# One inference step of a hybrid decoder on one core: a fifth staging place for the sample attention, and its third batch of keys staged with the first two

## The chip, the core and the metric

The kernel runs on one core of a Trainium2 chip. Its engines are named as in the profile: PE (TensorE, matrix products and transposes into PSUM), DVE (VectorE), ACT (ScalarE), POOL (GpSimd, here the issuer of gathers and of some loads) and SP (SyncE, here the issuer of the weight loads). They run in parallel, each in its own program order, and meet only at semaphores. The metric is the device time of one execution in microseconds; less is better.

## The reference

One layer of a decoder trunk for a prompt of 256 positions and for 8 sample rows of 4 new positions each: mixers, cross-attention, a mixture of experts. The change lies in the sparse attention of the sample rows. Each sample batch has 1024 cached positions in 8 pages, 2 key/value heads of 128, 8 query heads:

```python
def dsa_sample(q, k_new, v_new, qi, wi, ki_new, cache_k, cache_v, cache_idx_k, page_table, rel_bias):
    ...
    sc = indexer_scores(qi, wi, ki_all)
    sc = jnp.where(jnp.arange(n_keys)[None, None, :] <= qpos[None, :, None], sc, -jnp.inf)
    _, sel = lax.top_k(sc, topk)                      # 256 of the 1028 keys of each query
    ...
    k_sel = jnp.where(is_past, cache_k[phys, off], gather_rows(k_new, sn).astype(cache_k.dtype))
    v_sel = jnp.where(is_past, cache_v[phys, off], gather_rows(v_new, sn).astype(cache_v.dtype))
    rel_b = rel_bias[t5_bucket(qpos[None, :, None] - sel)]
    return sparse_attend(q, k_sel, v_sel, rel_b, valid)

def sparse_attend(q, k_sel, v_sel, rel_b, valid):
    ...
    logits = jnp.einsum('bqkgd,bqskd->bqkgs', qg, k_sel).astype(jnp.float32) * (Dh ** -0.5)
    logits = logits + rel_b...
    p = jax.nn.softmax(jnp.where(valid, logits, -jnp.inf), axis=-1).astype(v_sel.dtype)
    o = jnp.einsum('bqkgs,bqskd->bqkgd', p, v_sel)
```

The output of the attention goes, with the mixer's, into one output projection; cross-attention and the experts follow. All is in float32.

## The kernel before, in words

All work is written out by hand, engine by engine; there is no scheduler. PE runs the input projection in 12 items (`products(n)`, L711), with the prompt's attention and the indexer woven between its tiles (`INSIDE`, `AFTER`), then the sample attention, the output projection (L1023), the cross-attention, the router and the experts. SP loads the weights in the order of use, each into a place of a ring when PE has freed it.

The sample attention does not select keys: it computes the scores of all 1028 keys of a batch and adds a bias that holds the relative bias and, from the top-k rounds on DVE, a large negative value for keys not chosen. It works in two halves (`x` = 0, 1) of four batches:

- POOL gathers a batch's keys or values (128 x 2048 floats, 1 MB) from the paged cache into a staging place with an indirect DMA (`gather`, L584). There are four places of 2048 columns, `staged(b)` L333: two in `stageM`, two in `stageK`; batch b + 4 takes the place of batch b, and values 0 to 3 take the places of batches 4 to 7. Values 4 to 7 go to `vn_`, `qT_`, `qiT_` and `Kt` (L345), which are read by other work before; `qT_`, `qiT_` and `Kt` hold turned keys until the second half's scores are done. `stageK` lies in `nT`, the normed input, and is free when the last item's products are done.
- PE turns a batch's keys with 16 transposes of 128 x 128, in four groups of four (one PSUM bank each), and ACT (L1799) and DVE (L2181) copy two banks each to `keys_t(b)`. A group waits until its bank is copied out (`kt_free` counts ACT's copies, `kt_laid` DVE's, `kt_ready` PE's groups). Batches 0 and 1 are turned early, by `first_keys` (L870, transposes at L876), between the last steps of the last item (`AFTER[N_OUT - 1]`); their copies all go to DVE (L2156).
- PE computes the scores of four batches in PSUM (L979, releases `s_qk`), adds the bias (L986, releases `s_logits`; the first half waits for DVE's `topkS`). DVE takes the maximum (L2185), ACT the exponential (L1802, L1808), DVE scales and masks (L2190, L2191, releases `s_probs`).
- PE turns the probabilities (L996, L998) in banks 6 and 7, ACT copies them out (L1813, L1815), PE multiplies by the values (L1007, waits `v_in0`/`v_in1` for four gathers each; releases `s_o`), turns the result (L1013), and ACT lays it for the output projection (L1823). PE does this for half 0 and then half 1, after the scores of both.

POOL's order is one loop over b = 0 to 11 (keys of 8 batches, values of the first four): b = 2 waits for the last item's products (`ring_free`), b of 4 and more for the transposes of the batch whose place it takes, and the values of batch 4 go before b = 6. The last three gathers (values 5, 6, 7) wait for `s_qk` 2, the scores of both halves. Then POOL loads `xts` (L609, L611) and the memory keys. The tensor `nine` (4096 columns) holds the prompt's memory values in columns 0 to 1023 and is otherwise unused until the experts' ring takes it.

## Time and profile before

| | |
|---|---|
| three runs | 1218.6 us median (1215.48, 1218.6, 1225.76) |
| profiled execution | 1216.17 us; its span from first to last instruction 1214.3 us |
| busy in the span | PE 1131.3 us (93%), DVE 472.5, ACT 185.8, POOL 48.7 |
| chain that ended last, by engine | PE 79%, DVE 9%, DMA 7%, ACT 3% |
| of it, by line | L711 21%, L1023 15%, L1301 13%, DMA of `in_w_up` 5%, DMA of `in_cache_v` 1% |
| mean granted clock of TensorE | 0.977 |

The span has four stretches: the input projection with the prompt's attention up to 452 us; the sample attention, 452 to 497; output projection, cross-attention and router, 497 to 728, with a mean DMA share of 0.51; and the experts, 728 to 1204, with a DMA share of 0.99 at 415 GB/s. A row of the trace names start and duration in us, engine, line, operation, output and inputs by tile, partitions x elements, and in brackets the idle time of the engine before it and what released it. PE's matmul durations overlap; their ends are modelled.

### The profile page before, as it was taken

To read this page: it belongs to the slowest core of one execution; us is meant where nothing else is said; L and a number is where in the kernel's file an instruction comes from. 1 tells how busy PE (TensorE), PEld (TensorE's weight loads), DVE (VectorE), ACT (ScalarE), POOL (GpSimd) and SP (SyncE) were. 2 spreads that over 40 slices of the span, in tenths; PEclk is the share of its full clock that TensorE was granted. 3 is DMA by queue.
4 is the path that set the end of the run, shared out by engine and by line. 5 is a ranking of instruction groups with operands and counts; after the bars stand their busy time and mean duration, and the time that the engine had idled before them with its cause. 6 is when DMAs were issued, how large, how long until landed. Compare 5 with 4: busy or idle time off the path is not lost.

```text
span 1214.3 us, 14024 instructions
## 1 busy us (share of the span) xinstructions
PE 1131.3 (93%) x5834; PEld 557.4 (46%) x5834; DVE 472.5 (39%) x968; ACT 185.8 (15%) x399; POOL 48.7 (4%) x63
## 2 busy tenths in 40 slices
PE   7999999999999989899999899899999999859985
PEld 4334343344444455677777564333333333323332
DVE  5000069199564664011112466233333333412342
ACT  2103123200231343000012422000000000000010
POOL 0002000000000012100001001000000000000000
PEclk9999999999999999999999999899999999989998
DMA  8835623555343358744455739999999999999996
GB/s 292 294 122 136 190 73 124 191 174 173 109 134 104 109 206 320 291 136 137 138 171 184 286 119 405 399 412 426 428 426 427 427 426 427 426 426 428 425 427 245
DMA packets 71084, 327.60 MB, mean 270 GB/s; under 512 B 14006, under 2 KB 17878, under 8 KB 54444
## 3 DMA queue, kind: packets, MB, share of 16 engines
q1 hardware_dynamic: 55152, 282.65, 59.4%
q0 software_dynamic: 7888, 37.06, 8.1%
q10 hardware_dynamic: 7980, 6.99, 2.3%
q8 instruction: 47, 0.77, 0.3%
q14 instruction: 17, 0.14, 0.0%
HBM read 318.45 MB, written 10.49 MB: 271 GB/s over the span
## 4 chain that ended last, share of the span: by engine, by line
PE 79%; DVE 9%; DMA 7%; ACT 3%; issue 1%; POOL 0%; DVEq 0%; SPq 0%; ACTq 0%
PE PS L711 21%; PE PS L1023 15%; PE PS L1301 13%; PE PS L1383 7%; DMA ring<-in_w_up 5%; PE PS L1262 4%; PE PS L684 3%; PE PS L1308 2%; DVE X L2065 2%; DVE top L2064 2%; PE PS L1360 1%; PE PS L1266 1%; PE PS L1376 1%; DMA X<-in_cache_v,ids 1%; PE PS L705 1%
## 5 line engine op out<-in xcount | busy, mean ns | idle before, releaser
L711 PE MATMUL PS<-ring,NC 128*128 128x512 f32 x704 | 320.8, 600 | 1.8 <-issue 1.8
L711 PEld LDWEIGHTS PS<-ring,NC 128*128 128x128 f32 x704 | 128.7, 191 | 153.6 <-issue 152.0
L1023 PE MATMUL PS<-NC,ring 128*128 128x288 f32 x768 | 189.9, 407 | 1.6 <-DVE X L2223 0.5
L1301 PE MATMUL PS<-ring,NC 128*64 128x512 f32 x560 | 163.7, 605 | 7.7 <-DMA ring<-in_w_up 7.2
L1023 PEld LDWEIGHTS PS<-NC,ring 128*128 128x128 f32 x768 | 144.6, 190 | 42.4 <-issue 2.1
L2416 DVE TENSOR_TENSOR X<-X,PS 128x1024 f32<-128x1024 f32 x52 | 63.5, 1221 | 119.0 <-PE PS L1262 119.0
L1301 PEld LDWEIGHTS PS<-ring,NC 128*64 128x64 f32 x560 | 46.2, 138 | 101.6 <-issue 100.1
L1262 PE MATMUL PS<-XNN,NC 64*128 64x512 f32 x208 | 58.8, 642 | 1.4 <-DVE XNN L2454 0.8
L2223 DVE TENSOR_TENSOR X<-X,PS 128x288 f32<-128x288 f32 x16 | 7.3, 454 | 117.9 <-PE PS L1023 117.9
L1308 PE MATMUL PS<-ring,NC 128*32 128x256 f32 x384 | 35.8, 449 | 16.5 <-DMA ring<-in_w_up 14.9
L1909 ACT ACTIVATE NC<-PS,small 64x512 f32<-64x512 f32 x11 | 7.5, 680 | 273.6 <-PE PS L1301 239.7
L2064 DVE MAX8 top<-X 32x8 f32<-32x1028 f32 (+2 forms) x48 | 44.7, 931 | 1.0
L2065 DVE MATCH_REPLACE8 X<-top,X 32x1028 f32<-32x1028 f32 (+2 forms) x48 | 43.9, 914 | 0.0
L2419 DVE TENSOR_TENSOR X<-X,PS 32x1024 f32<-32x1024 f32 x26 | 31.5, 1210 | 26.6 <-PE PS L1266 26.4
L2091 DVE TENSOR_TENSOR ring<-small,cst 128x128 f32<-128x128 f32 x1 | 0.3, 293 | 105.1 <-ACT small L1636 105.1
L1383 PE MATMUL PS<-ring,NC 128*64 128x512 f32 x176 | 39.4, 595 | 0.0
L684 PE MATMUL PS<-ring,NC 128*32 128x512 f32 x288 | 38.4, 605 | 0.0
L1308 PEld LDWEIGHTS PS<-ring,NC 128*32 128x32 f32 x384 | 18.1, 128 | 34.7 <-issue 29.8
L1262 PEld LDWEIGHTS PS<-XNN,NC 64*128 64x128 f32 x208 | 15.8, 186 | 39.5 <-issue 25.6
L2454 DVE COPY XNN<-PS 128x1024 f32<-128x1024 f32 x11 | 13.5, 1225 | 44.6 <-PE PS L1383 32.1
L1830 ACT ACTIVATE NC<-X,gcol 128x288 f32<-128x288 f32 x16 | 8.6, 535 | 117.0 <-DVE X L2223 117.0
L630 POOL DMA_INDIRECT NC<-nsc,tabS x13 | 13.0, 1002 | 331.1 <-PE PS L1253 281.6
(454 smaller groups left out, 1178.5 us busy)
## 6 DMA issues: line engine op xcount, KB each, us to landing
ring<-in_w_gate SPq DMA_DIRECT2D x27, 2048.0 KB, 20.0
ring<-in_w_up SPq DMA_DIRECT2D x22, 2048.0 KB, 17.1
ring<-in_w_in SPq DMA_DIRECT2D x36, 1024.0 KB, 5.1
ring<-in_w_down SPq DMA_DIRECT2D x16, 2048.0 KB, 18.5
ring<-in_w_out SPq DMA_DIRECT2D x16, 1024.0 KB, 5.1
nine<-in_w_down SPq DMA_DIRECT2D x6, 2048.0 KB, 22.1
XNN<-in_w_up SPq DMA_DIRECT2D x5, 2048.0 KB, 18.9
NC<-in_w_gate SPq DMA_DIRECT2D x5, 2048.0 KB, 20.8
```

What stands on the lines that cost most here:

```text
L684: last = mm(acc(n, 2)[32 * k:32 * k + 32, 0:width], lhs[:, 4 * q + k, T:NT], ws[:, k, 0:width], start=st, stop=sp_)
L711: last = mm(acc(n, t)[:, 0:width], lhs[:, kt, t * 128:(t + 1) * 128], slot(m)[:, k, 0:width], start=kt == 0, stop=kt == KT - 1)
L1023: last = mm(PS[:, j, 0:NT], slot(m)[:, k, 128 * j:128 * j + 128], src[:, kt, :], start=kt == 0, stop=kt == width * 4 - 1)
L1262: last = mm(PS[:, banks + half, :], slot_w[rows, k, 128 * t:128 * t + 128], ysb[rows, k, 512 * x:512 * x + 512], start=True, stop=True)
L1301: last = mm(PS[64 * half:64 * half + 64, 2, :], x[:, kt % 8, kt // 8, :], weights[half][:, kt % 8, :], start=kt == 0, stop=kt == KT - 1)
L1308: last = mm(PS[32 * c:32 * c + 32, bank, 0:256], x[:, kt % 8, kt // 8, STRIP * sub:STRIP * sub + STRIP], weights[c // 2][:, kt % 8, 256 * ...
L1383: last = mm(PS[64 * half:64 * half + 64, bank + x, :], hT[:, f, :], w[:, f % 2, half * 1024 + x * 512:half * 1024 + x * 512 + 512], start= ...
L2064: own(V.max(best, work))
L2065: own(V.match_replace(work, best, work, TAKEN))
L2416: return TT(out, out, PS[:, banks:banks + 2, :], ALU.add)
L2419: last = TT(out, out, PS[32 * x:32 * x + 32, banks:banks + 2, :], ALU.add)
L2454: V.tensor_copy(ysb[:, block_of(p) % 2, :], PSF[:, 2048:3072]).then_inc(S("y_out_psum"), 1)
```

## The change

- `KV_PLACES`: five staging places instead of four; the new one is `nine[:, 1024:3072]`. Key batch j takes place j % 5, the values of batches 0 to 3 take the next ones, and values 5 take the place in `nine`, 6 and 7 take `qT_` and `qiT_`; `Kt` holds no values any more.
- POOL gathers three batches of keys before it waits for `ring_free`, in the order keys 0 to 7, values 0 to 3, values 5; each from the sixth on waits for the transposes of the batch five before it. Keys 7 count on the semaphore `idx_in`. Two gathers (values 6, 7) are left behind `s_qk` 2.
- `first_keys(2)` turns the third batch between the fold of the last item and that item's transposes. Its four groups go to ACT. So the loop of the stage has one batch less in the first half.
- `turn_probs(x)` is the code of the probability transposes as a function; that of half 0 runs before the scores of half 1, after a wait for all DVE key copies (`kt_laid` 18).

```diff
@@ -332,9 +332,11 @@
...
+        KV_PLACES = (stageM[:, 0:2048], stageM[:, 2048:4096], nine[:, 1024:3072], stageK[:, 0:2048], stageK[:, 2048:4096])
+
         def staged(b):
...
-            return (stageM, stageK)[b % 4 // 2][:, 2048 * (b % 2):2048 * (b % 2) + 2048]
+            return KV_PLACES[b % 5]
@@ -342,7 +344,7 @@
...
-            return staged(b) if b < 4 else (vn_, qT_, qiT_, Kt)[b - 4]
+            return staged(8 + b) if b < 4 else (vn_, staged(12), qT_, qiT_)[b - 4]
@@ -588,20 +590,22 @@
...
-            for b in range(12):
-                if b == 2:
+            for j in range(13):
+                if j == 3:
                     pool.wait_ge(S("ring_free"), 4 * N_OUT)
-                if b == 6:
+                if j >= 5:
+                    pool.wait_ge(S("kt_ready"), 4 * (j - 4))
+                if j < 8:
+                    gather(staged(j), ck, j, f"k_in{j % 4}" if j < 7 else "idx_in")
+                elif j < 12:
+                    gather(values(j - 8), cv, j - 8, "v_in0")
+                else:
+                    gather(values(5), cv, 5, "v_in1")
+                if j == 7:
                     pool.wait_ge(S("misc_free"), groups_through(("item", N_OUT - 1)))
                     gather(values(4), cv, 4, "v_in1")
-                if b >= 4:
-                    pool.wait_ge(S("kt_ready"), 4 * (b - 3))
-                if b < 8:
-                    gather(staged(b), ck, b, f"k_in{b % 4}")
-                else:
-                    gather(values(b - 8), cv, b - 8, "v_in0")
             pool.wait_ge(S("s_qk"), 2)
-            for b in (5, 6, 7):
+            for b in (6, 7):
                 gather(values(b), cv, b, "v_in1")
@@ -866,11 +870,12 @@
...
                 pe.wait_ge(S("acc_out"), N_OUT - 1)
-                pe.wait_ge(S(f"k_in{b}"), 16)
                 for c in range(2):
...
                         g = 4 * b + 2 * c + half
-                        if g >= 2:
+                        if g >= 10:
+                            pe.wait_ge(S("kt_free"), g - 9)
+                        elif g >= 2:
                             pe.wait_ge(S("kt_laid"), g - 1)
@@ -932,10 +937,14 @@
...
                     pe.wait_ge(S("cst_in"), 16)
+                if n == N_OUT - 1:
+                    for b in range(3):
+                        pe.wait_ge(S(f"k_in{b}"), 16)
                 products(n)
...
                         fold(N_OUT - 1)
+                        first_keys(2)
                     if isinstance(what, str):
@@ -950,29 +959,47 @@
...
                 if g >= 2:
-                    pe.wait_ge(S("kt_free"), 12 + g - 1)
+                    pe.wait_ge(S("kt_free"), 14 + g - 1)
                 return PS[:, 6 + g % 2, :]
...
                 if g >= 4:
-                    pe.wait_ge(S(("kt_free", "kt_laid")[g % 2]), (0, 8)[g % 2] + (g - 4) // 2 + 1)
+                    pe.wait_ge(S(("kt_free", "kt_laid")[g % 2]), (4, 8)[g % 2] + (g - 4) // 2 + 1)
                 return PS[:, 4 + g % 4, :]
+            def turn_probs(x):
+
+                pe.wait_ge(S("s_probs"), x + 1)
+                for g in range(3):
+                    bank = kgroup()
+                    if g < 2:
+                        for i in range(4):
+                            r = 4 * g + i
+                            last = tr(bank[:, i * 128:i * 128 + 128], PB[:, x, 128 * r:128 * r + 128], ident)
+                    else:
+                        last = tr(bank[0:R, 0:128], PN[:, x * 32:x * 32 + 32], ident)
+                    last.then_inc(S("kt_ready"), 1)
             for x in range(2):
                 four = range(4 * x, 4 * x + 4)
-                for b in four[2 if x == 0 else 0:]:
-                    pe.wait_ge(S(f"k_in{b % 4}"), 16 * (x + 1))
+                for b in four[3 if x == 0 else 0:]:
+                    if b < 7:
+                        pe.wait_ge(S(f"k_in{b % 4}"), 16 * (x + 1))
+                    else:
+                        pe.wait_ge(S("idx_in"), 16 * 9)
                     for c in range(2):
                         for half in range(2):
-                            bank = key_bank(4 * (b - 2) + 2 * c + half)
+                            bank = key_bank(4 * (b - 3) + 2 * c + half)
                             for i in range(4):
...
                             last.then_inc(S("kt_ready"), 1)
-                pe.wait_ge(S("kt_free"), 8 * x + 4)
+                pe.wait_ge(S("kt_free"), 8 * x + 6)
                 pe.wait_ge(S("kt_laid"), 8)
+                if x:
+                    pe.wait_ge(S("kt_laid"), 18)
+                    turn_probs(0)
                 for i, (a, z) in enumerate(KEYCUT):
                     if i == 1:
-                        pe.wait_ge(S("kt_laid"), 8 * x + 12)
+                        pe.wait_ge(S("kt_laid"), 8 * x + 10)
                     for c in range(2):
@@ -987,17 +1014,9 @@
...
             for x in range(2):
-                pe.wait_ge(S("s_probs"), x + 1)
-                for g in range(3):
-                    bank = kgroup()
-                    if g < 2:
-                        for i in range(4):
-                            r = 4 * g + i
-                            last = tr(bank[:, i * 128:i * 128 + 128], PB[:, x, 128 * r:128 * r + 128], ident)
-                    else:
-                        last = tr(bank[0:R, 0:128], PN[:, x * 32:x * 32 + 32], ident)
-                    last.then_inc(S("kt_ready"), 1)
-                pe.wait_ge(S("kt_free"), 12 + groups[0])
+                if x:
+                    turn_probs(1)
+                pe.wait_ge(S("kt_free"), 14 + groups[0])
                 pe.wait_ge(S(f"v_in{x}"), 16 * 4)
@@ -1012,7 +1031,7 @@
...
                 last.then_inc(S("kt_ready"), 1)
-            pe.wait_ge(S("kt_free"), 12 + groups[0])
+            pe.wait_ge(S("kt_free"), 14 + groups[0])
             pe.nop().then_inc(S("moe_free"), 2)
@@ -1773,6 +1792,9 @@
...
                         folded(N_OUT - 1)
+                        for g in range(8, 12):
+                            act.wait_ge(S("kt_ready"), g + 1)
+                            A(keys_t(2)[:, g // 2 % 2, 512 * (g % 2):512 * (g % 2) + 512], PS[:, g % 2, :], ACT.Copy).then_inc(S("kt_free"), 1)
                     if isinstance(what, str):
@@ -1790,12 +1812,12 @@
...
             act.preload_act_table(ACT.Exp)
-            for b in range(2, 8):
+            for b in range(3, 8):
                 if b == 4:
...
                 for c in range(2):
-                    g = 4 * (b - 2) + 2 * c
-                    act.wait_ge(S("kt_ready"), 8 + g + 1)
+                    g = 4 * (b - 3) + 2 * c
+                    act.wait_ge(S("kt_ready"), 12 + g + 1)
                     A(keys_t(b)[:, c, 0:512], PS[:, 4 + g % 4, :], ACT.Copy).then_inc(S("kt_free"), 1)
@@ -2176,8 +2198,8 @@
...
                 for c in range(2):
-                    g = 4 * (b - 2) + 2 * c + 1
-                    dve.wait_ge(S("kt_ready"), 8 + g + 1)
+                    g = 4 * (b - 3) + 2 * c + 1
+                    dve.wait_ge(S("kt_ready"), 12 + g + 1)
                     V.tensor_copy(keys_t(b)[:, c, 512:1024], PS[:, 4 + g % 4, :]).then_inc(S("kt_laid"), 1)
@@ -2190,8 +2212,7 @@
...
                    cc("newmask")[:, x * 32:x * 32 + 32].rearrange("p (b s) -> p b s", b=8), ALU.mult).then_inc(S("s_probs"), 1)
-            for b in range(2, 4):
-                lay_keys(b)
+            lay_keys(3)
             sample_max(0)
...
             lay_keys(5)
```

How the order of instructions moves, at three places. A name before `<-` is written, those behind it are read; `ring` holds most staging places here, `NC` the two of `stageK`, `nine` the new one.

PE at the end of the last item, before. L739 folds the item's partial sums, L770 and L774 turn the item, L969 turns keys of the third and fourth batch:

```order
L739 MATMUL PS<-XNN,cst 32x128 [waits misc_free,part]
L739 MATMUL PS<-XNN,cst 32x128 x3
L770 MATMUL PS<-cst,XNN 128x128 [waits misc_free,normed]
L770 MATMUL PS<-cst,XNN 128x128 x3
L770 MATMUL PS<-cst,XNN 128x128 [waits misc_free]
L770 MATMUL PS<-cst,XNN 128x128 x3
L774 MATMUL PS<-cst,natS 128x128 [waits misc_free]
L969 MATMUL PS<-cst,NC 128x128 [waits k_in2,acc_out,misc_free]
L969 MATMUL PS<-cst,NC 128x128 x15
```

The same place in the changed kernel:

```order
L743 MATMUL PS<-XNN,cst 32x128 [waits misc_free,part]
L743 MATMUL PS<-XNN,cst 32x128 x3
L881 MATMUL PS<-cst,nine 128x128 [waits kt_laid,acc_out]
L881 MATMUL PS<-cst,nine 128x128 x3
L881 MATMUL PS<-cst,nine 128x128 [waits kt_laid]
L881 MATMUL PS<-cst,nine 128x128 x3
L881 MATMUL PS<-cst,nine 128x128 [waits kt_free]
L881 MATMUL PS<-cst,nine 128x128 x3
L881 MATMUL PS<-cst,nine 128x128 [waits kt_free]
L881 MATMUL PS<-cst,nine 128x128 x3
L774 MATMUL PS<-cst,XNN 128x128 [waits misc_free,normed]
L774 MATMUL PS<-cst,XNN 128x128 x3
```

The third batch's four groups (L881, from `nine`) now stand between the fold (now L743) and the item's own transposes (now L774); of the 32 transposes of L969 (now L993) 16 are left behind them.

PE between the last keys and the values, before: the second half's scores (L979) and bias (L986), then the turn of the first half's probabilities (L996, L998), then the first values:

```order
L979 MATMUL PS<-X,ring 32x512
L979 MATMUL PS<-ring 32x512 x2
L979 MATMUL PS<-X,ring 32x512 x2
L979 MATMUL PS<-ring 32x512 x2
L979 MATMUL PS<-kTs,ring 32x4 x8
L986 MATMUL PS<-ring,cst 32x512 x8
L986 MATMUL PS<-ring,cst 32x4 x4
L996 MATMUL PS<-cst,XNN 128x128 [waits s_probs]
L996 MATMUL PS<-cst,XNN 128x128 x7
L998 MATMUL PS<-cst,PN 32x128 [waits kt_free]
L1007 MATMUL PS<-ring,XNN 32x256 [waits v_in0,kt_free]
```

In the changed kernel, from the last keys (L993) on:

```order
L993 MATMUL PS<-cst,nine 128x128 [waits kt_free]
L993 MATMUL PS<-cst,nine 128x128 x3
L993 MATMUL PS<-cst,nine 128x128 [waits kt_laid]
L993 MATMUL PS<-cst,nine 128x128 x3
L978 MATMUL PS<-cst,XNN 128x128 [waits kt_laid,s_probs,kt_free]
L978 MATMUL PS<-cst,XNN 128x128 x7
L980 MATMUL PS<-cst,PN 32x128 [waits kt_free]
L1006 MATMUL PS<-X,ring 32x512 x2
L1006 MATMUL PS<-ring 32x512 x2
L1006 MATMUL PS<-X,ring 32x512 x2
```

The turn (now L978, L980) stands before the second half's scores (now L1006) and behind a wait for the keys' copies and the probabilities; behind the bias the values (now L1026) follow at once.

POOL, the gathers, before:

```order
L584 DMA ring<-in_cache_k,ids 128x2048 x2
L584 DMA NC<-in_cache_k,ids 128x2048 [waits ring_free]
L584 DMA NC<-in_cache_k,ids 128x2048
L584 DMA ring<-in_cache_k,ids 128x2048 [waits kt_ready] x2
L584 DMA ring<-in_cache_v,ids 128x2048 [waits misc_free]
L584 DMA NC<-in_cache_k,ids 128x2048 [waits kt_ready] x2
L584 DMA ring<-in_cache_v,ids 128x2048 [waits kt_ready] x2
L584 DMA NC<-in_cache_v,ids 128x2048 [waits kt_ready] x2
L584 DMA ring<-in_cache_v,ids 128x2048 [waits s_qk]
L584 DMA ring<-in_cache_v,ids 128x2048
L584 DMA X<-in_cache_v,ids 128x2048
```

And in the changed kernel:

```order
L586 DMA ring<-in_cache_k,ids 128x2048 x2
L586 DMA nine<-in_cache_k,ids 128x2048
L586 DMA NC<-in_cache_k,ids 128x2048 [waits ring_free]
L586 DMA NC<-in_cache_k,ids 128x2048
L586 DMA ring<-in_cache_k,ids 128x2048 [waits kt_ready] x2
L586 DMA nine<-in_cache_k,ids 128x2048 [waits kt_ready]
L586 DMA ring<-in_cache_v,ids 128x2048 [waits misc_free]
L586 DMA NC<-in_cache_v,ids 128x2048 [waits kt_ready] x2
L586 DMA ring<-in_cache_v,ids 128x2048 [waits kt_ready] x2
L586 DMA nine<-in_cache_v,ids 128x2048 [waits kt_ready]
L586 DMA ring<-in_cache_v,ids 128x2048 [waits s_qk]
L586 DMA ring<-in_cache_v,ids 128x2048
```

One gather of keys moves ahead of the wait for `ring_free`, and two instead of three stand behind the wait for `s_qk`.

## Rows read from the trace of the kernel before

**Rows 1.** The chain of waits, 452 to 622 us: start, duration, what.
```profile
452.94 4.90 PE PS L969 x28
458.51 3.74 PE PS L979 x45
462.25 1.89 PE PS L986 x21
...
472.17 3.82 PE PS L979 x45
479.08 11.08 DMA X<-in_cache_v,ids
490.29 5.96 PE PS L1007 x72
497.67 124.41 PE PS L1023 x512
```

**Rows 2.** The timeline, last key copy to the second turn.
```profile
471.96 0.69 DVE L2181 COPY ring<-PS 128x512 f32<-128x512 f32 x1 [0.18 <-PE PS L969]
...
478.62 1.23 DVE L2185 TENSOR_REDUCE small<-PS 128x1 f32<-128x1028 f32 x1 [5.97 <-PE PS L986]
...
480.71 1.09 ACT L1808 ACTIVATE XNN<-PS,small 128x1028 f32<-128x1028 f32 x1
...
481.39 0.41 PE L1007 MATMUL PS<-ring,XNN 128*32 128x256 f32 x2 [1.10 <-DMA NC<-in_cache_v,ids]
...
482.93 0.19 DVE L2191 TENSOR_TENSOR PN<-XNN,cst 128x32 f32<-128x32 f32 x1
...
485.54 1.09 PE L996 MATMUL PS<-cst,XNN 128*128 128x128 f32 x8
...
487.21 0.27 ACT L1815 ACTIVATE XNN<-PS 32x128 f32<-32x128 f32 x1
```

**Rows 3.** The timeline, POOL's gathers: start, duration, engine, line, what, idle before.
```profile
441.01 0.94 POOL L584 DMA_INDIRECT NC<-in_cache_k,ids  x1 [215.01 <-PE PS L684]
...
466.31 0.94 POOL L584 DMA_INDIRECT ring<-in_cache_v,ids  x1 [6.84 <-PE PS L969]
...
476.58 0.94 POOL L584 DMA_INDIRECT ring<-in_cache_v,ids  x1 [3.45 <-PE PS L979]
```

**Rows 4.** Windows of 2 us: busy per engine, then PE clock, DMA share, GB/s.
```profile
466.00:468.00 2.00, 1.82 (x18) 1.61 (x17) 1.63 (x4) 2.00 (x5) 0.94 (x1) 1.00 0.20 29
...
476.00:478.00 2.00, 2.00 (x26) 0.78 (x19) 0.00 (x0) 0.00 (x0) 1.11 (x2) 1.00 1.04 438
...
480.00:482.00 2.00, 0.90 (x13) 0.59 (x17) 0.07 (x1) 1.83 (x4) 0.01 (x1) 1.00 0.97 348
...
490.00:492.00 2.00, 1.71 (x20) 1.13 (x24) 0.00 (x0) 0.00 (x0) 0.57 (x1) 0.60 0.03 8
492.00:494.00 2.00, 2.00 (x28) 1.30 (x24) 0.00 (x0) 0.00 (x0) 0.00 (x0) 0.54 0.96 249
```

**Rows 5.** The gathers by their index tile, 380 to 520 us: issue to landing.
```profile
DMA to landing us min/median/max: 6.3/8.5/11.1
```

**Rows 6.** Windows of 3 us, columns as in rows 4.
```profile
234.00:237.00 3.00, 3.00 (x8) 1.15 (x7) 0.00 (x0) 0.00 (x0) 0.00 (x0) 1.00 0.38 161
```

**Rows 7.** The timeline, end of the last item and the stage's head.
```profile
448.49 0.43 PE L739 MATMUL PS<-XNN,cst 128*32 128x128 f32 x8
...
450.90 1.09 PE L770 MATMUL PS<-cst,XNN 128*128 128x128 f32 x8 [1.98 <-DVE natS L2060]
...
452.90 1.28 ACT L1792 ACT_TABLE_LOAD   x1
...
454.20 0.60 ACT L1799 ACTIVATE ring<-PS 128x512 f32<-128x512 f32 x1
...
455.14 0.48 DVE L2173 MEMSET gh<- 128x512 f32 x1 [0.17 <-issue]
```

**Rows 8.** Waits of SP's queue, 400 to 780 us: line, releaser, us, times, longest.
```profile
SPq L531 <- PE PS L1023: 206.0, 20, 64.5
```

## The prediction

> **What bounds the kernel now.** I read the chain of waits first. The program runs on one core, and the stage that the change touches stands alone in it: the attention of the sample rows, from 452.9 to 497.7 us [rows 1]. There the chain runs over TensorE (PE): key transposes (L969), scores (L979), bias (L986), keys again, scores again. Then it leaves PE: 11.08 us of it is one gather of values, issued at 479.08 and landed at 490.16. Only then do the second half's value products (L1007) run, and the output projection (L1023) after them. The reader is to see that this gather ends last, not PE: PE's probability transposes for that half were done at 487.2 [rows 2], so PE stood idle for 3.1 us.
>
> The queue of the gathers (POOL) says why. The first value gather goes out at 466.31 and the first of the last three at 476.58, when the second scores are done [rows 3]. In the windows almost nothing moves from 466 to 468, and 438 GB/s at 476 to 478 [rows 4]. So the queue is dry at 466, then works through seven gathers of 1 MB from about 468.2 to 490.16: 22.0 / 7 = **3.14 us each**. From issue to landing they take 6.3 to 11.1 us, 8.5 in the median [rows 5]. The last landing is late because the queue was idle before 468 and has seven to do after.
>
> PE's clock stands in the same windows [rows 4]: granted 1.00 (2.4 GHz) at 480 to 482, but 0.60 and 0.54 right after the idle 3.1 us, so partly 1.2 GHz. The second half's value products take 5.96 us [rows 1] for work that the first half, started at 481.39, finished before the transposes of 485.54 [rows 2]: 4.15 us.
>
> **Part 1: the third batch's keys early.** They are gathered near 226, right behind the first two batches, instead of at 441.01 [rows 3]. That is 1 MB more at 228 to 237, where the three microseconds after 234 show a DMA share of 0.38 [rows 6]; 2.4 us of transfer fit there and no chain step waits on it. Cost 0, hidden by the weight blocks being loaded ahead; without that cover it would cost at most the 3.1 us of one gather.
>
> Their 16 transposes now come after the fold of the last item (ends 448.92) and before that item's own transposes, which today start at 450.90 because they wait for VectorE (DVE) [rows 7]. So two microseconds of PE are free there. Four groups of four at 1.09 / 8 us each [rows 7] are 0.55 us a group; ScalarE (ACT) evicts each in 0.60 us [rows 7], and groups three and four wait for it: PE is through at 451.4, ACT at 452.0. Behind ACT's four copies stand its copies for the last item, so those end about 0.5 us later, and PE enters the stage at 453.4 instead of 452.94. What stays there is one batch: 16 transposes at 4.90 / 28 us [rows 1], 2.8 us. ACT has its table load of 1.28 us first [rows 7], then two copies, the second once its group is there at 455.5: done at 456.1. DVE is free at 455.62 (its memset) [rows 7] and makes its two copies, 0.69 us each [rows 2], by 457.0; only the second score block needs them. The scores start at 456.2 instead of 458.51: **2.3 us earlier**, and all up to the last key copy moves with them, the bias included (DVE wrote its mask before the memset of 455.14, earlier than needed).
>
> **Part 2: the first half's probabilities turned before the second scores.** Today DVE's last key copy starts at 471.96 and ends at 472.65 [rows 2], and the second scores start at 472.17 [rows 1]. Now PE first waits for all DVE key copies (the turned rows use the same banks), at 472.65 - 2.3 = 470.4, and then turns eight tiles and a small one. The same work for the other half started at 485.54; ACT's last copy of it starts at 487.21 and ends at 487.48 [rows 2], so PE takes 1.67 us. The scores start at 472.1 and end, with 3.82 us, at 475.9, where today they end at 475.99 [rows 1]. So this move gives back all of part 1's gain at this point: queued behind the added wait are the scores, and behind them the release of POOL's last gathers. What it buys is behind: the first half's value products can follow the bias directly, 478.3 to 482.4, if their values are there, and ACT's exponential of the second half no longer stands behind the copies of the first. DVE delivers the second probabilities today at 483.12 [rows 2]; the maximum of the logits was there at 479.85 and the exponential began at 480.71 [rows 2], so with ACT free it is 0.9 us earlier, 482.2. The second turn then takes 482.5 to 484.4 (1.94 us as today).
>
> **Part 3: the gathers.** Every value gather of the first half is released one batch earlier: the first at 456.3 (third place of the five, freed when batch three is turned) instead of 466.31, the other three about 2.3 us before today's predecessors. One of the second half's, batch five, goes out after the last key transposes, near 470, instead of after the scores. After the scores only **two** are left, at 476.5 and 477.8, not three. On the queue: four gathers (values 1, 2, 3, 5) from 464.0 on, data from 466.0, then these two, never dry for long: 466.0 + 6 x 3.14 = **484.9 us** for the last, against 490.16. The keys of batch seven wait for the early transposes and go out at 451.5, before today's 458, so they are not late.
>
> **The sum.** The second value products need PE's operands (484.4) and the gather (484.9): start at 485.0. PE idles 0.6 us instead of 3.1, so I take the 4.15 us of the full clock: end at 489.2, where today it is 496.2. Gain **7.0 us**: 5.3 by the earlier landing, 1.7 by the clock.
>
> Behind this stage I carry it whole. The 512 products at L1023 run 124.41 us without a gap [rows 1], and SP's weight loads wait for PE (206.0 us in total for L1023) [rows 8], so they move with it. The expert stage is bound by its weight stream, but its first loads also wait for PE in program order, so its start moves too.
>
> Against the profiled execution (1216.2 us) that gives 1209.2; against the median of the three runs (1218.6) 1211.6. I forecast the middle, **1210.5 us**.
>
> **Bounds of what no row shows.** The last landing is the unknown. From its issue at 477.8: the shortest 6.3 us gives 484.1, below PE's own 484.4, so the gain is at most 7.5; the median 8.5 gives 486.3, and a gain of 5.7 at full clock, 4.0 if the clock drops again; the longest, 11.1, gives 488.9, the low clock for certain, and a gain of 1.4. I take 484.9, since the queue carries six and not seven. The head of the stage is worth 1.8 to 2.7 by how ACT's copies fall; part 2 absorbs an error there one for one only if it delays the scores' end.
>
> **The rule weighed.** A drained queue would be faster than my 3.14 us: the row at 476 shows 438 GB/s, by which 1 MB is 2.4 us. The Trainium skill, page "DMA: Bandwidth & Descriptors", section "Anatomy of one DMA — SWDGE (gpsimd) path", puts a transfer of this queue at a fixed 2.0 us plus its bytes at 436 GB/s, an estimate of 4.4 us for one gather of 1 MB. By that rule the trace's 6.3 us minimum would be queueing, and the last landing near 482.2.
>
> **Rivals.**
> 1. *The gather leaves the path.* If a gather that finds its queue nearly empty needs only a start of 2 us (issue 466.31, data from 468.2) and 2.4 us of transfer, the last lands at 477.8 + 4.4 = 482.2, and PE's chain (exponential, probabilities, second turn) decides at 484.4: gain 7.5, 1210.0 on my base. For it: the 438 GB/s. Against: no landing under 6.3. The rule of the page named above gives this outcome. Chance 0.25.
> 2. *Latency, not backlog.* If the 8.5 to 11.1 us belong to the gather itself, two instead of three saves only one issue of 1.25 us and part of the clock: gain 1.4 to 4.0, time 1213.5 to 1216. For it: the last gather took 11.08 with the queue already flowing. Against: 3.14 us apiece fits all seven. Chance 0.12.
> 3. *The gain is taken back behind.* If something not released by PE set the expert stream's start, nothing is left: 1217.5. Against: [rows 8]. Chance 0.05.
> 4. *Slower: the clock.* The new order has short waits of PE at 452, 470 and 472. From the scores at 472.0 to the end there are 3.8 + 2.0 + 4.15 + 1.6 + 4.15 = 15.7 us of full-clock work. If the clock fell to 1.2 GHz at 470 and stayed there it would take 31.4: 15.7 lost against 7.0 won, 1226. It decides from 14 us of such work at the low level. Against: at 480 to 482 PE was busy 0.90 of 2 us at 1.00 [rows 4]. Chance 0.03.
>
> My forecast, a gain of 4 to 7.3, has 0.55.
>
> **Numbers.** The range: the gain of 7.5 below the lowest run (1215.5) is 1208.0, and the runs before scatter by some us on either side, so 1205.5 below; the smallest gain, 1.4, below the median is 1217.2, so 1217.5 above. It leaves out rival 4, half of rival 3 and scatter. One per cent, 12 us, is about what a measurement can tell from no change. No case gains that; only scatter could: 0.05. Slower by it: rival 4 at its full price, 0.02. Within: 0.93.
>
> **What will show it.** In the profile after: scores of the first half starting at 456 and the second half's at 472; two gathers, not three, after 476; the last landing at 485 (over 487 is rival 2, under 483.5 with PE waiting for probabilities is rival 1); the second value products in about 4.2 us at clock 1.00; the output projection starting near 490.7 instead of 497.67, and the same distance from there to the end. A stream of expert weights that starts at today's time, or scores of the second half ending after 478, would make me wrong.

## The result: 0.5% faster, in the stage that was forecast, with some steps right for the wrong reason

| | before | changed |
|---|---|---|
| median of 13 runs each, us | 1220.3 (1215.5 to 1226.7) | 1214.2 (1206.5 to 1221.1) |
| ratio, with its 95% interval | | 0.9947 [0.9922, 0.9972] |
| profiled execution, us | 1216.2 | 1210.5 |
| start of the last fold to start of the output projection, us | 49.1 | 42.2 |

The forecast was 1210.5 us and a gain of 7.0. The medians differ by 6.1 us, the interval of the ratio is a gain of 3.4 to 9.5 us. That the profiled execution took 1210.5 us is luck at this scatter.

Runs of one kernel lie 11 to 15 us apart and follow the mean clock that TensorE was granted: the changed kernel's fastest, 1206.5, had 0.981 and its slowest, 1221.1, had 0.970. The start of the stage scatters too, by 6.5 us over the runs told of here. So the experiments are read by a distance inside the trace: from the start of the last item's fold (448.56 in the kernel before, the chain's piece behind rows 7) to the start of the output projection (497.67 [rows 1]). I call it the **stage distance**. Two runs of the changed kernel give 42.19 and 41.88.

The chain of waits of the changed kernel, start, duration, what; the fold is L743, scores L1006, the turn L978 and L980, values L1026, projection L1042:

```profile
448.66 0.36 PE PS L743 x8
...
455.71 3.74 PE PS L1006 x45
...
470.11 0.64 PE PS L978 x4
...
471.71 3.75 PE PS L1006 x45
...
476.96 8.07 DMA ring<-in_cache_v,ids
...
485.16 4.27 PE PS L1026 x72
...
490.85 124.41 PE PS L1042 x512
```

Against [rows 1]: the first scores start 2.80 us earlier, the second 0.46 us earlier. The last landing is at 485.03 instead of 490.16, the second value products take 4.27 us instead of 5.96, and the projection starts 6.82 us earlier. POOL's gathers in the timeline, against [rows 3]:

```profile
451.71 0.93 POOL L586 DMA_INDIRECT nine<-in_cache_k,ids  x1 [2.29 <-PE PS L881]
...
463.51 0.93 POOL L586 DMA_INDIRECT NC<-in_cache_v,ids  x1 [6.92 <-PE PS L993]
...
469.74 0.95 POOL L586 DMA_INDIRECT nine<-in_cache_v,ids  x1 [1.43 <-PE PS L993]
475.71 0.94 POOL L586 DMA_INDIRECT ring<-in_cache_v,ids  x1 [5.03 <-PE PS L1006]
```

The windows, columns as in [rows 4] (near the end: clock, DMA share, GB/s):

```profile
452.00:454.00 2.00, 1.33 (x10) 0.90 (x9) 1.93 (x4) 1.98 (x5) 1.12 (x2) 1.00 0.99 393
...
476.00:478.00 2.00, 2.00 (x36) 0.93 (x32) 0.00 (x0) 0.00 (x0) 1.59 (x2) 1.00 0.70 205
...
486.00:488.00 2.00, 2.00 (x45) 1.45 (x38) 0.00 (x0) 0.00 (x0) 0.17 (x1) 1.00 0.71 128
```

The clock stays at 1.00 where it had been 0.60 and 0.54 behind the idle time. And at 476 to 478 the queue moves 205 GB/s, not 438: it had run nearly dry. That speaks against a step of mine, below. PE's own chain, in the timeline:

```profile
482.01 0.19 DVE L2213 TENSOR_TENSOR PN<-XNN,cst 128x32 f32<-128x32 f32 x1
...
483.92 0.27 ACT L1837 ACTIVATE XNN<-PS 32x128 f32<-32x128 f32 x1
```

The second probabilities come at 482.20 and their turn is copied at 484.19, so the landing ends last by 0.8 us.

Behind the stage the lead is 6.8 us at 683.2 and 7.0 us at the last weights, and 5.7 at the end. What is missing lies in the last expert's products, which in this execution took 5.04 us against 3.67. The trace of the changed kernel, then that of the kernel before:

```profile
1182.75 5.41 PE PS L1327 x64
1190.89 5.04 PE PS L1379 x32
```

```profile
1189.76 5.41 PE PS L1308 x64
1197.95 3.67 PE PS L1360 x32
```

An unchanged tail took 5.06 us in the fifth experiment, 5.10 in the sixth, whose code there is that of the kernel before. So that is scatter, not a thing given back.

### The profile page after: what moved, and what is told of

It reads as the page before. It is cut to its first block, busy times and chain, and to the rows that moved or that the text cites. A ratio compares the mean times of both kernels' runs of the same rounds, so it can differ in the third digit from the quotient of the medians.

```text
span 1208.6 us, 14025 instructions
## 1 busy us (share of the span) xinstructions
PE 1131.5 (94%) x5834; PEld 555.5 (46%) x5834; DVE 471.1 (39%) x966; ACT 186.6 (15%) x401; POOL 48.8 (4%) x63
## 4 chain that ended last, share of the span: by engine, by line
PE 80%; DVE 9%; DMA 6%; ACT 4%; issue 1%; DVEq 0%; POOL 0%; SPq 0%; ACTq 0%
PE PS L715 21%; PE PS L1042 16%; PE PS L1320 13%; PE PS L1402 7%; DMA ring<-in_w_up 5%; PE PS L1281 4%; PE PS L688 3%; PE PS L1327 2%; DVE X L2087 2%; DVE top L2086 2%; PE PS L1379 1%; PE PS L1285 1%; PE PS L1395 1%; PE PS L709 1%; DMA X<-in_x_prompt 1%
## 5 line engine op out<-in xcount | busy, mean ns | idle before, releaser
L1042 PE MATMUL PS<-NC,ring 128*128 128x288 f32 x768 | 189.9, 407 | 1.6 <-DVE X L2244 0.5
L1042 PEld LDWEIGHTS PS<-NC,ring 128*128 128x128 f32 x768 | 144.6, 190 | 42.4 <-issue 1.2
L1281 PEld LDWEIGHTS PS<-XNN,NC 64*128 64x128 f32 x208 | 15.9, 187 | 39.5 <-issue 25.6
```

Of the source, the lines that this page charges most:

```text
L1042: last = mm(PS[:, j, 0:NT], slot(m)[:, k, 128 * j:128 * j + 128], src[:, kt, :], start=kt == 0, stop=kt == width * 4 - 1)
L1281: last = mm(PS[:, banks + half, :], slot_w[rows, k, 128 * t:128 * t + 128], ysb[rows, k, 512 * x:512 * x + 512], start=True, stop=True)
```

## The experiments

All stage distances:

```
                                            fold     projection  distance
before                                      448.56   497.67      49.11
changed                                     448.66   490.85      42.19
changed, once more                          449.07   490.95      41.88
1 turn of the probabilities late            450.61   491.34      40.73
  the same, timed                           446.30   487.34      41.04
2 values 5 late                             451.58   499.48      47.90
3 third keys gathered late                  449.73   491.95      42.22
4 third keys turned late                    452.19   499.61      47.42
5 before, PE kept busy                      445.68   492.69      47.01
6 before, values 5 early                    445.70   491.96      46.26
7 all values early                          451.32   491.99      40.67
8 all values early, turn before the bias    451.32   490.96      39.64
```

**1. The turn back behind the second scores.**

```diff
-                if x:
-                    pe.wait_ge(S("kt_laid"), 18)
-                    turn_probs(0)
...
-                if x:
-                    turn_probs(1)
+                turn_probs(x)
```

> The changed kernel with the first half's probabilities turned behind the second half's scores, as before; all else as changed. The measure is the start of the output projection: 497.67 us before, 490.85 in the changed kernel. My theory: the move of the turn only trades places. The second scores start near 470.1 and end near 473.9 instead of 475.5, the last two gathers go out at 474.0 and 475.2 and land at 483.3 to 484.3, but PE's own chain is later: turn until 477.8, ACT's last copy, values of half 0 from 479.0 to 483.2, second turn to 485.1. The second value products start at 485.1 (485.16 now) and the projection at 490.5 to 491.2. Rival (the moved turn is where the gain came from): the projection starts 1.5 us or more later, at 492.4 or after.

The chain of this kernel (fold, second scores, turn, values of either half); the start of the projection is in the table, here and below:

```profile
450.61 0.35 PE PS L743 x8
...
471.32 3.74 PE PS L1003 x45
...
476.95 1.24 PE PS L978 x8
...
479.50 4.22 PE PS L1022 x72
...
485.65 4.27 PE PS L1022 x72
```

Neither theory: the distance is 1.46 us shorter than in the changed kernel. The second scores start 20.7 us after the fold (23.05 in the changed kernel), so the last gather goes out at 476.64, 26.0 after it instead of 28.3. PE reached the second value products by its own chain, 35.0 after the fold; the changed kernel waits there for the landing until 36.5. The last gather landed 8.9 us after its issue, at 485.5, so landing and chain came together there. I had PE's chain 1.4 us too slow (second value products 36.4 after the fold). The same kernel, timed:

> The kernel of the first experiment again (the changed kernel with the turn of the first half's probabilities behind the second scores), timed. I count from the start of the last item's fold, since that start scatters by some us from run to run, to the start of the output projection: 49.1 us before, 42.2 and 41.9 in two runs of the changed kernel, 40.7 in the first experiment. Theory: the move of the turn costs 1.5 us, so 40.7 again (40.4 to 41.1), and 8.4 us less than before: ratio 0.9931. Rival (the 1.5 us were scatter): 41.9 to 42.3.

```profile
446.30 0.35 PE PS L743 x8
...
472.33 9.19 DMA ring<-in_cache_v,ids
481.66 4.27 PE PS L1022 x72
```

41.04: the direction holds, with 0.8 to 1.5 us by this pair and the two traces of the changed kernel. Now the landing (35.2 after the fold) ends last again, just. The timed ratio to before is 0.9959 [0.9934, 0.9985], which can't be told from the changed kernel's.

**2. Values 5 behind the second scores again.**

```diff
-            for j in range(13):
+            for j in range(12):
...
-            for b in (6, 7):
+            for b in (5, 6, 7):
                 gather(values(b), cv, b, "v_in1")
```

> The changed kernel with the values of batch 5 gathered again behind the second scores: three gathers there and not two, everything else as changed. Queue theory (3.14 us for each of the gathers that are left): the three go out at 475.7, 477.0 and 478.2, data from 477.7, the last lands at 487.1 to 487.8; PE idles 3 us and its clock may fall, so the second value products take 4.2 to 5.9 us and the projection starts at 492.8 to 495. Latency rival (a gather costs only its issue of 1.25 us, and lands 8.07 us after it): landing 486.3, projection at 492.1. Third: if the last landing is not what ends last, nothing changes: 490.9.

```profile
481.65 9.41 DMA ring<-in_cache_v,ids
491.20 6.86 PE PS L1024 x72
```

```profile
490.00:496.00 6.00, 4.80 (x48) 2.62 (x52) 0.00 (x0) 0.00 (x0) 0.58 (x1) 0.50 0.50 159
```

5.7 us lost. The three gathers went out from 479.15 on and landed after 11.9 us; the two of the changed kernel after 9.3, from 475.71. So on a drained queue one gather more is 2.6 us. The rest of the later landing is 0.5 us of issue. Both together are 3.1 us, clear of the scatter: the landing is 39.5 us after the fold here, and 36.1 to 36.4 in the three traces that issue these gathers as the changed kernel does. And the clock was 0.50 (1.2 GHz) behind PE's wait of 4.2 us, so the products took 6.86 us: 2.6 us more. Here the one gather costs twice, once as transfer and once as clock.

**3. Third batch gathered late, turned early.**

```diff
-                if j == 3:
+                if j == 2:
                     pool.wait_ge(S("ring_free"), 4 * N_OUT)
```

> The changed kernel with the third batch's keys gathered only when the last item's products are done (at 441), with a semaphore of their own, but turned at the changed place. Theory: they land 6.3 to 8.5 us after 441.1, at 447.4 to 449.6, just when PE wants them at 449.0, and the gathers behind are one later with slack; the projection starts 0 to 1 us later than 490.85. Rival (the early gather is needed): PE waits for the landing with the 4 groups' copies, 2 us or more, and the projection starts at 493 or later.

```profile
449.73 0.36 PE PS L743 x8
450.08 0.60 PE PS L881 x4
```

42.22, as in the changed kernel: the early gather is worth nothing in this stage. The third batch, issued at 441.5, is there when PE wants it: its transposes (L881) follow the fold at once.

**4. Third batch gathered early, turned in the stage.** `first_keys(2)` and ACT's copies for it are taken out, the loops start at batch 2 again and the counts follow.

```diff
                     if what == ("item", N_OUT - 1):
                         fold(N_OUT - 1)
-                        first_keys(2)
```

> The changed kernel with the third batch's keys gathered early but turned in the stage, with the fourth, as before. Theory: the head of the stage loses what I counted for it: first scores at 458.4 instead of 455.7, all behind 2.3 to 2.8 us later, the last two gathers go out at 478.3 and 479.6, land near 487.6, PE's chain ready near 487; projection at 493.2 to 493.7. Rival (the head is hidden, since another thing ends last): projection at 490.9 to 491.5. If the clock falls in the head again, as it did before at 452 to 456, up to 1 us more than the theory's loss.

```profile
452.19 0.40 PE PS L743 x8
...
463.19 3.74 PE PS L1005 x45
...
484.44 8.01 DMA ring<-in_cache_v,ids
492.58 5.62 PE PS L1025 x72
```

```profile
456.00:460.00 4.00, 3.45 (x17) 2.93 (x16) 3.61 (x6) 2.93 (x5) 0.00 (x0) 0.50 0.70 285
```

5.2 us lost. The first scores start 11.0 us after the fold (7.05 in the changed kernel, 9.95 before), at a clock of 0.50 in 456 to 460; the landing is 3.9 us later with them, and the products lose 1.35 us more.

The head shows what the early turn does for the clock. In the four traces without it (the kernel before, the fourth, fifth and sixth experiments) the granted clock falls to 0.50 behind PE's idle time there; in the eight with it, it stays at 1.00. The low stretch was longer here than in the kernel before (6.8 us against 3.4), with the same order of work in the head, so about 1 us of the 5.2 is that.

The slow products are another matter. The wait before them, here and then in the changed kernel, and the windows here:

```profile
492.58 0.61 PE L1025 MATMUL PS<-ring,XNN 128*32 128x256 f32 x1 [1.22 <-DMA ring<-in_cache_v,ids]
```

```profile
485.16 0.38 PE L1026 MATMUL PS<-ring,XNN 128*32 128x256 f32 x1 [1.27 <-DMA ring<-in_cache_v,ids]
```

```profile
490.00:492.00 2.00, 1.10 (x9) 0.68 (x7) 0.00 (x0) 1.50 (x4) 0.00 (x0) 0.99 0.42 176
492.00:494.00 2.00, 1.42 (x16) 0.84 (x20) 0.00 (x0) 0.00 (x0) 0.57 (x1) 0.50 0.04 8
```

PE waited 1.22 us and the clock fell to 0.50; in the changed kernel it waited 1.27 us, with the turn before it at the same distances, and the clock stayed at 1.00. So this drop is not explained by a longer wait, and its cause stays open. The 1.35 us can't be booked to the late turn.

**5. The kernel before with PE kept busy in the idle time.**

```diff
+                if x:
+                    for i in range(20):
+                        tr(PS[:, 2, i % 4 * 128:i % 4 * 128 + 128], ident, ident)
                 pe.wait_ge(S(f"v_in{x}"), 16 * 4)
```

> The kernel before with 20 transposes of the identity (into a bank that nobody reads) between the second turn of the probabilities and the wait for the last values, where PE idles for 3.1 us. Nothing is left out. Clock theory: PE keeps its full clock, the second value products take 4.2 us instead of 5.96, and the projection starts at 496.0 instead of 497.67. Rival (the products are slow for another reason: their operands lie elsewhere, the transfers beside them): 5.9 us and 497.7 as before.

```profile
484.67 2.40 PE PS L1003 x20
487.07 4.20 PE PS L1010 x72
```

POOL's load behind the last landing:

```profile
486.44 0.58 POOL L609 DMA_DIRECT2D X<-xts  x1 [9.36 <-DMA X<-in_cache_v,ids]
```

The same products on the same operands take 4.20 us and not 5.96, at a clock of 1.00: the clock theory holds, with 1.76 us, and the rival of the operands is out. That the added work is what kept the clock, this trace can't show. POOL starts this load 0.57 us behind the landing in the kernel before and in the changed one (490.72 behind 490.16, 485.59 behind 485.03), so the last values landed near 485.9 here and PE would have waited only 1.4 us.

That landing is 40.2 us after the fold, where the kernel before has 41.6, with the same gathers issued at the same distances from the fold (the last 30.5 us after it in both). So **the landing of this code scatters by 1.4 us**. The added transposes, which ended about 1.1 us after it, took most of that back: 0.3 of the 2.1 us gained.

**6. The kernel before with values 5 early, that part alone.**

```diff
-            return staged(b) if b < 4 else (vn_, qT_, qiT_, Kt)[b - 4]
+            return staged(b) if b < 4 else (vn_, nine[:, 1024:3072], qT_, qiT_)[b - 4]
...
+            gather(values(5), cv, 5, "v_in1")
             pool.wait_ge(S("s_qk"), 2)
-            for b in (5, 6, 7):
+            for b in (6, 7):
...
```

> The kernel before with one part of the change alone: the values of batch 5 go to the unused columns of the tensor of the memory values, right behind the first half's values (near 473.5), so that two gathers and not three stand behind the second scores. Queue theory: the queue has seven gathers from 468.2 on, as before, so the last lands at 490.2 again and the projection starts at 497.7 (497.3 to 497.8). Latency rival: the last goes out 1.25 us earlier, at 477.8, and lands 8.1 to 11.1 us later, at 485.9 to 488.9; projection at 493 to 496.4.

```profile
445.70 0.40 PE PS L740 x8
...
474.70 11.44 DMA ring<-in_cache_v,ids
486.28 4.27 PE PS L1008 x72
```

The landing is 40.4 us after the fold, 41.6 in the kernel before: 1.2 us earlier, the latency rival's issue step of 1.25 us. But the fifth experiment, with the gathers of before, landed at 40.2. So the two theories can't be told apart here, and whether this part alone brings the landing forward is not shown. The distance falls by 2.85, of which 1.69 us is the clock: PE idles 2.4 us and it stays at 1.00.

**7. All values before the second scores.** Values 6 and 7 go to `X[:, 4096:6144]` (the top-k work) and to `NAT` (the items' block), free by then. POOL's loads of `xts` go behind the value products.

```diff
-            pool.wait_ge(S("s_qk"), 2)
-            for b in (6, 7):
-                gather(values(b), cv, b, "v_in1")
-            pool.wait_ge(S("s_logits"), 2)
+                    gather(values(7), cv, 7, "v_in1")
+                if j == 8:
+                    pool.wait_ge(S("topkS"), 1)
+                    gather(values(6), cv, 6, "v_in1")
...
```

> The changed kernel with values 6 and 7 gathered at 454 to 457 too, into columns that are free by then (the prompt block of the last items, and the columns of the top-k work), so that no gather stands behind the second scores; the load of the saved input moves behind the value products. Theory: the transfer leaves the path and PE's chain (maximum, exponential, probabilities, second turn, ready at 484.2) decides: the second value products start at 484.3 instead of 485.16 and the projection at 490.0, 0.8 us earlier than in the changed kernel; against the kernel before 7.6 us, a ratio of 0.9938. Rival: more gathers in the queue at 455 to 470 delay keys or the first half's values, and the projection starts at 491 or later.

```profile
470.02 10.00 DMA ring<-in_cache_v,ids
480.16 4.22 PE PS L1026 x72
...
486.30 4.27 PE PS L1026 x72
```

40.67: 1.2 to 1.5 us shorter, more than the 0.8 expected. The first half's values, behind two gathers that are wanted later, land at 480.02 and hold PE for 0.26 us; the second value products follow by PE's chain. What the theory missed is DVE's maximum of the second half, in the changed kernel and here:

```profile
478.52 1.23 DVE L2207 TENSOR_REDUCE small<-PS 128x1 f32<-128x1028 f32 x1 [8.67 <-PE PS L1013]
```

```profile
480.00 1.23 DVE L2207 TENSOR_REDUCE small<-PS 128x1 f32<-128x1028 f32 x1 [7.51 <-PE PS L1013]
```

It starts 3.2 us after the bias products start in the changed kernel (475.31) and 2.05 here (477.95). With PE's wait for the second probabilities (0.84 us in the changed kernel) gone, its chain is 0.5 us shorter. The start is 2.8 to 3.2 us after the bias in the ten traces in which gathers go out beside it, and 2.05 in the two, this one and the eighth's, in which none does; why is not shown. Timed: 0.9961 [0.9938, 0.9983]. Beside it the changed kernel ran again:

> The changed kernel once more, beside the last one on the same chip, so that the two are timed against the same runs of the kernel before. Theory: 6.8 us less than before in the stage and nothing given back: ratio 0.9944, projection at 490.85. Rival: a part is given back behind the stage: the distance from the start of the projection to the end is longer than the 716.6 us of before by more than the scatter of the clock.

0.9954 [0.9933, 0.9974], with 720.2 us from the projection to the end in its profile, 717.8 in the first, 716.6 before. The other traces have 716.4 to 723.4 there; the two longest are 723.0, the fifth experiment's, with the tail of before, and 723.4, the eighth's, with the new one. So nothing that I can tell from scatter is given back.

**8. All values early in the order of use, the turn between scores and bias.**

```diff
+            return (staged(8), NAT[:, 0:2048], X[:, 4096:6144], staged(9), vn_, staged(10), staged(11), staged(12))[b]
...
                 last.then_inc(S("s_qk"), 1)
+                if x:
+                    turn_probs(0)
```

> The changed kernel with two edits. All value gathers go out before the second scores: values 1 and 2, which are wanted first, at 454 to 458 into columns that are free by then, values 0, 3, 5, 6, 7 into the five places as the keys leave them, so that nothing is queued ahead of the first half's values. And the turn of the first half's probabilities stands between the second scores and their bias, where ACT's copies of it lie beside the bias. Counted from the start of the last fold to the output projection (42.2 in the changed kernel, 40.7 with the turn late, both with PE waiting 1.3 us for ACT's copies before each value product): the first such wait falls away, the second stays, and no gather ends last: 39.3 to 39.9, ratio to before 0.9923. Rival 1 (bandwidth: 13 MB of gathers keep the queue busy until 478, as with all values early, where the first value products began 28.8 us after the fold): 40.5 to 41. Rival 2 (the bias 1.3 us later delays the softmax, which then ends last): 40.5 to 41.5, with PE waiting for DVE before the second turn.

```profile
472.02 3.74 PE PS L1003 x45
...
477.32 1.89 PE PS L1012 x21
479.21 4.16 PE PS L1025 x72
...
485.28 4.27 PE PS L1025 x72
```

39.64, as expected: the first values follow the bias at once, and no gather is in the chain from the second scores on. It is the shortest stage, 9.5 us less than before. In time it is 0.9964 [0.9936, 0.9992]: faster than before, and not to be told from the changed kernel. At 15 us of scatter its 2.5 us can't be shown so; whether they reach the end stays open.

## Why the prediction was right, point by point

- **Part 1, early gather: 0.** Right; the third experiment shows that it isn't even needed.
- **Part 1, early turn: 2.3 us.** It was 2.8, and 3.95 when taken out of the changed kernel, where the low clock lasted longer. Under-sized: I counted transposes and copies, but not that the head had PE at 0.61 of its clock from 452 to 456, which the filled idle time ended.
- **Part 2, the moved turn.** Its price at the second scores was right in kind (their lead fell from 2.8 to 0.46 us). That it buys something behind was wrong: taken back, the stage is 0.8 to 1.5 us shorter. With the turn late, the second scores release the last gathers 2.3 us earlier, they land 1.2 to 1.5 us earlier (34.9 and 35.2 after the fold, 36.4 in the changed kernel), and PE's own chain is there by then too.
- **Part 3, the last landing at 484.9.** Measured 485.03, but the working failed: "never dry for long: 466.0 + 6 x 3.14". The queue did run nearly dry before the last two. They went out 0.8 us earlier than I had, the first landed 6.8 us later and the second 2.5 us behind it. The 3.14 us is a rate for a queue with seven in it; that the gap it leaves out and the earlier start cancelled is luck. Rival 2 had the first part of the truth (issue time and latency), and its price was too high since it took a loaded queue's 8.5 to 11.1 us for an empty one's.
- **Rival 1**, 4.4 us for a gather on a drained queue: no landing that the traces have between 380 and 520 us is under 5.5 us. The estimate of 4.4 us from the Trainium skill's page "DMA: Bandwidth & Descriptors", section "Anatomy of one DMA — SWDGE (gpsimd) path", was short here by 1.1 us at the least.
- **The clock: 1.7 us.** Right for the changed kernel: 4.27 us in both its traces, and the fifth experiment shows that the length of these products goes with the clock. Rival 4 did not come: none of its short waits cost clock. But the fourth experiment lost it behind a wait of 1.22 us, so the term was less certain than I had it.
- **Carried whole to the end.** Right within what can be told: 6.8 us in the stage, 6.1 in the medians.

The sum of parts doesn't add. Taken out one at a time they cost 5.7 (values 5), 5.2 (the turn of the keys), 0 and -1.5: the first two alone are more than the whole 6.9. Both hold slow clock besides the work moved: 2.6 us of the first, behind PE's wait of 4.2 us, and about 2.4 of the second, 1 in the head and 1.35 in the products, of which the last may be scatter.

## What to carry to other kernels

Where a transfer ends last before a stage, count first what is issued behind the last release: one piece more there cost 3.1 us of landing in the second experiment. An idle time of PE that is taken away can give more than its length, since the work behind it no longer runs at the low clock; read the granted clock beside the wait. Take each part of a change out again: one of those tried here cost time, one did nothing. And know the scatter of the step that you read: the same gathers landed 1.4 us apart in two traces, more than the sixth experiment looked for.

## What the runs showed of the hardware

PE at full clock waited 3.1 us before the second value products and found 0.60, 4.2 us in the second experiment and found 0.50, 2.4 us in the sixth and found 1.00; but 1.22 us in the fourth and found 0.50. So the length of the last wait alone does not tell. The indirect gathers of 1 MB took 5.5 us at the least from issue to landing, 2.5 to 2.6 us for each more on a drained queue, 3.0 to 3.14 us each with seven queued. A gather's issue on POOL took 0.94 us, but 1.57 and 1.82 where DVE wrote its mask beside it (453.15 in the kernel before, 453.53 in the changed one). In the fourth experiment the same gather (values 4) went out at 462.55, 4 us behind the mask, and its issue took 0.94 us. The Trainium skill, page "SBUF — State Buffer", section "Who interferes with whom", has DVE's two-port operations lock GpSimd out while descriptors are written; the traces fit it, with 0.6 to 0.9 us, though none shows that the mask ran in such a mode.
